# A decoder layer on one core: projections in two halves of the tokens, with the gated recurrence woven into them

## The reference

```python
h = rmsnorm(x, norm_gain) * (1 + scale[:, None]) + shift[:, None]
qa, ka, va, za, qb, fb, ib, zb, ga, gb = jnp.split(h @ w_in, cuts, axis=-1)
# branch A: dilated window attention, three groups (dilation 1, 4, 16), with RMS-normed q and k
branch_a = (o_a * jax.nn.silu(za)) @ w_ba
# branch B: gated recurrence, 4 heads, forget dim 128, value dim 128
f = lbh + (1.0 - lbh) * jax.nn.sigmoid(fb)
o_b, s_new = hgrn2_recurrence(jax.nn.silu(qb), 1.0 - f, ib, jnp.log(f), hgrn_state)
branch_b = (rmsnorm(o_b, o_gain) * jax.nn.silu(zb)) @ w_bb
merged = jax.nn.sigmoid(ga) * branch_a + jax.nn.sigmoid(gb) * branch_b
y = x + gate[:, None] * (merged @ w_o)
```

## Time and profile before

| | us |
|---|---|
| median of 3 runs | 3477.08 |
| profiled execution | 3473.88 |
| its span | 3472.1 |
| PE busy / DVE / ACT / POOL | 3033.0 / 1518.9 / 840.6 / 679.0 |
| mean granted clock of PE | 0.925 |

### The profile page before, as it was taken

One profiled execution on the slowest core, in us unless ns is written; L12 is line 12 of the kernel. 1 busy time (PEld: TensorE's weight loads), 2 busy tenths in 40 slices (PEclk: granted clock), 3 DMA queues, 4 the chain that ended last, 5 costly groups with the idle time before them and its releaser, 6 DMA issues. The chain is left out here.

```text
span 3472.1 us, 45359 instructions
## 1 busy us (share of the span) xinstructions
PE 3033.0 (87%) x17964; PEld 2737.5 (79%) x17964; DVE 1518.9 (44%) x2895; ACT 840.6 (24%) x1646; POOL 679.0 (20%) x662
## 2 busy tenths in 40 slices
PE   7499999999999999999999689898555566569999
PEld 7499999999999999999998456666344545459999
DVE  2687111111111114876666334343466766644343
ACT  1311000013333332111111345344222222222010
POOL 0311111024454543111110002112022222222000
PEclk9999999999999999999999799897777767779999
DMA  5212223221212212221221868767322020035333
GB/s 178 91 59 75 75 57 76 64 69 63 78 66 78 83 55 90 75 75 59 75 72 51 304 222 263 259 210 255 112 88 76 1 76 26 1 124 166 111 120 97
DMA packets 246786, 362.19 MB, mean 104 GB/s; under 512 B 22704, under 2 KB 183728, under 8 KB 230192
## 3 DMA queue, kind: packets, MB, share of 16 engines
q1 hardware_dynamic: 239664, 350.64, 31.4%
q10 hardware_dynamic: 6912, 8.65, 0.7%
HBM read 237.45 MB, written 121.79 MB: 103 GB/s over the span
## 5 line engine op out<-in xcount | busy, mean ns | idle before, releaser
L495 PE MATMUL project_bank<-h_high,project_w_high 128*128 128x448 f32 (+1 forms) x2240 | 795.0, 355 | 28.3 <-POOL project_w_low L585 28.3
L496 PE MATMUL project_bank<-h_low,project_w_high 128*128 128x448 f32 (+1 forms) x2240 | 794.8, 355 | 0.0
L497 PE MATMUL project_bank<-h_high,project_w_low 128*128 128x448 f32 (+1 forms) x2240 | 794.7, 355 | 0.0
L495 PEld LDWEIGHTS project_bank<-h_high,project_w_high 128*128 128x128 f32 x2240 | 421.3, 188 | 53.7 <-issue 28.4
L496 PEld LDWEIGHTS project_bank<-h_low,project_w_high 128*128 128x128 f32 x2240 | 421.1, 188 | 25.5
L497 PEld LDWEIGHTS project_bank<-h_high,project_w_low 128*128 128x128 f32 x2240 | 421.1, 188 | 24.9
L585 POOL TENSOR_TENSOR project_w_low<-project_w_raw,project_w_high 128x512 fp32r<-128x512 f32 x144 | 185.0, 1290 | 771.6 <-ACT project_w_high L539 771.6
L509 PE MATMUL project_bank<-project_w_high,h_low 128*128 128x256 f32 x1088 | 307.9, 283 | 0.0
L508 PE MATMUL project_bank<-project_w_low,h_high 128*128 128x256 f32 x1088 | 307.9, 283 | 0.0
L507 PE MATMUL project_bank<-project_w_high,h_high 128*128 128x256 f32 x1088 | 307.9, 283 | 0.0
L642 DVE SCALAR_TENSOR_TENSOR project_out<-project_bank,project_gains,project_rstd 128x448 f32<-128x448 f32 (+2 forms) x120 | 89.0, 742 | 404.0 <-ACT project_rstd L556 404.0
(11 more groups left out here) (188 smaller groups left out, 4642.7 us busy)
## 6 DMA issues: line engine op xcount, KB each, us to landing
mix_kv<-in_kT_c SPq DMA_DIRECT2D x24, 1024.0 KB, 7.5
mix_kv<-in_v_c SPq DMA_DIRECT2D x24, 1024.0 KB, 7.1
project_w_raw<-in_w_qkv SPq DMA_DIRECT2D x72, 256.0 KB, 4.9
scratch_gates<-project_out SPq DMA_DIRECT2D x16, 1056.0 KB, 4.5
tail_gates<-scratch_gates SPq DMA_DIRECT2D x48, 352.0 KB, 3.2
scratch_sums<-mix_o_out SPq DMA_DIRECT2D x48, 264.0 KB, 6.0
mix_rows<-scratch_sums SPq DMA_DIRECT2D x24, 528.0 KB, 7.0
scratch_v_rows<-project_out SPq DMA_DIRECT2D x24, 520.0 KB, 6.8
```

Source lines behind the costliest of these rows:

```text
L495: pe.matmul(dst, w_high[:, s, k, :], h_high[:, k, tok], start=(k == 0), stop=False)
L496: pe.matmul(dst, w_high[:, s, k, :], h_low[:, k, tok], start=False, stop=False)
L497: mm = pe.matmul(dst, w_low[:, s, k, :], h_high[:, k, tok], start=False, stop=(k == KD - 1))
```

## The change

The features of half of the tokens are in SBUF at a time (`h_high` and `h_low` have 1088 columns in the place of 2112). phase_input makes the second half first and stores it to DRAM (`store_h`, two DMAs for each of three chunks, six in all, 8.9 MB), then the first half over it; ACT, DVE and POOL wait for the stores whose columns they write over.

`phase_weave` takes the place of phase_project and of phase_hgrn, which is gone. It runs the list of jobs twice, once for each half of the tokens, in chunks of 512 or of 384, 352 and 352 columns, two jobs of a weight pair taking turns; the weights are loaded and split in each half. Between the halves SP loads the stored features (`load_features`). The first 14 jobs of a half are those that feed the recurrence. From then on each unit has a slot number, and at each slot every engine does, after its part of the unit, what `recurrence(s, k)` has for it: a step s of the recurrence begins every 13 slots (9 after a sample step) and is spread over slots -5 to 17 counted from its start. All operations of the recurrence and their shapes stay; its inputs go through DRAM as before. Its PSUM needs four banks; the banks of the projections are 3 in the place of 5, those of the head sums 1 in the place of 2. POOL's cast of the squares goes to DVE (`high_squares`), DVE's reciprocal to ACT: the curve is now exp(-log(1 + exp(-u))), with DVE's clamp and maximum around it. q and k of the dilations 4 and 16 are stored by SP in pieces of 256 or 64 elements (`by_group`), since each half has only a part of each residue's row.

```diff
+    CHUNK = ((1024, 384), (1408, 352), (1760, 352), (0, 352), (352, 336), (688, 336))
...
+                def store_h(c):
+                    sp.wait_ge(low_a_done, c + 1)
+                    sp.wait_ge(low_b_done, c + 1)
+                    sp.dma_start(dr["h_half"][0, :, :, cols(c)], h_high[:, :, cols(c)].bitcast(F32)).then_inc(h_stored[c], 16)
+                    sp.dma_start(dr["h_half"][1, :, :, cols(c)], h_low[:, :, cols(c)].bitcast(F32)).then_inc(h_stored[c], 16)
...
                     load_x(c)
+                    store_h(c - XBUF)
...
+def phase_weave(nc, t, dr):
...
+    HALF = SEQ // 2
+    CHUNKS_OF = (((0, 512), (512, 512)), ((1024, 384), (1408, 352), (1760, 352)))
+    ORDER = ([("query", 0, 0), ("forget", 0, 0), ("query", 1, 0), ("forget", 1, 0), ("input", 0, 0), ("z", 4, 0), ("z", 5, 0),
+              ("query", 2, 0), ("forget", 2, 0), ("query", 3, 0), ("forget", 3, 0), ("input", 1, 0), ("z", 6, 0), ("z", 7, 0)]
+             + [("value", g, m) for m in range(2) for g in range(G)]
+             + [(kind, g, jp) for jp in range(PAIRS) for g in range(G) for kind in ("q", "k")]
+             + [("z", n, 0) for n in range(4)] + [("gate", b, m) for m in range(8) for b in range(2)])
+    FIRST_JOBS = 14
+    JOBS = [(half, *job) for half in range(2) for job in ORDER]
     ROWS, NORMED, CURVED = ("value", "input"), ("q", "k"), ("query", "forget", "z", "gate")
-    RAW, RING, BANKS = 3, 3, 5
+    RAW, RING, BANKS = 3, 5, 3
...
+    HSTEPS = [(h, j) for h in range(BH) for j in (0, 1)] + [(h, j) for h in range(BH) for j in (2, 3, 4)]
+    LEVELS = [7 if j < 4 else 3 for h, j in HSTEPS]
...
+        T0 = []
+        for s, (h, j) in enumerate(HSTEPS):
+            if s in (0, 2 * BH):
+                T0.append(5 if s == 0 else HALF_SLOTS + 5)
+            else:
+                T0.append(T0[-1] + (13 if big(s - 1) else 9))
+        END = T0[-1] + 14
...
+            return [(s, T - T0[s]) for s in range(len(HSTEPS)) if -5 <= T - T0[s] <= 17]
...
+            return [4 * (pair + 1) + i for i in ((0, 1), (2,), (3,))[pos]] if pos < 3 and pair + 1 < NPAIR else []
 
...
+                def load_features(c):
+                    lo, w = CHUNKS_OF[1][c][0] - HALF, CHUNKS_OF[1][c][1]
+                    last = pair_first[NPAIR // 2] - (2 if c == 0 else 0)
+                    sp.wait_ge(unit_done, last)
+                    sp.dma_start(h_high[:, :, lo:lo + w].bitcast(F32), dr["h_half"][0, :, :, lo:lo + w]).then_inc(h_in[c], 16)
+                    sp.dma_start(h_low[:, :, lo:lo + w].bitcast(F32), dr["h_half"][1, :, :, lo:lo + w]).then_inc(h_in[c], 16)
...
+                    by_group = lambda dst: dst.rearrange("p (r x) -> p r x", r=DIL[x])[:, :, lo // DIL[x]:(lo + HALF) // DIL[x]]
+                    rows = lambda src: src[:, 0:HALF].rearrange("p (r x) -> p r x", r=DIL[x])
...
-                        sp.dma_start(dr["qT_s"][y, x], a[:, SEQ:NT]).then_inc(done, 16)
+                        sp.dma_start(by_group(dr["qT"][x, y]), rows(a)).then_inc(done, 16)
...
+                    for p in pieces_at(U):
+                        if p + 3 < 2 * len(WEIGHTS):
+                            load(p + 3)
+                    if U == pair_first[NPAIR // 2] - 2:
+                        load_features(0)
+                    if U == pair_first[NPAIR // 2] - 1:
+                        load_features(1)
+                        load_features(2)
+                    if U in slot_of:
+                        for s, k in active(slot_of[U]):
+                            recurrence(s, k)
...
-                for U, (j, u) in enumerate(STEPS):
-                    if u == 0:
-                        pe.wait_ge(w_low_done, 2 * (TILE[j] + (2 if JOBS[j][0] in ROWS else 1)))
+                pe.wait_ge(const_in, 112)
+                for U, (j, c) in enumerate(STEPS):
+                    half, kind = JOBS[j][:2]
+                    if U == pair_first[pair_of(U)]:
+                        pe.wait_ge(w_low_done, 4 * (pair_of(U) + 1))
+                    if U - pair_first[NPAIR // 2] in (0, 2, 4):
+                        pe.wait_ge(h_in[(U - pair_first[NPAIR // 2]) // 2], 32)
                     if U >= BANKS:
                         pe.wait_ge(evac_done, U - BANKS + 1)
-                    if JOBS[j][0] in ROWS:
+                    if kind in ROWS:
...
+                    if U and is_a("normed", U - 1):
                         head_sums(U - 1)
+                    if U in slot_of:
+                        for s, k in active(slot_of[U]):
+                            recurrence(s, k)
...
+                def logarithm(U):
+                    n, e = NTH["curved", U], curve_part(U)
+                    act.wait_ge(clamp_done, n + 1)
+                    act.activation(e, e, ACT.Exp, scale=-1.0).then_inc(eu_done, 1)
+                    act.wait_ge(eu_done, n + 1)
+                    act.activation(e, e, ACT.Ln, bias=1.0).then_inc(log1_done, 1)
+                def sigmoid(U):
+                    n, e = NTH["curved", U], curve_part(U)
+                    act.wait_ge(larger_done, n + 1)
+                    act.activation(e, e, ACT.Exp, scale=-1.0).then_inc(sig_done, 1)
...
+                for U in range(len(STEPS)):
+                    if is_a("normed", U):
                         square(U)
-                    elif JOBS[j][0] in CURVED:
-                        exponential(U)
-                    if U and normed(U - 1):
+                    if is_a("curved", U):
+                        logarithm(U)
+                    if U and is_a("normed", U - 1):
                         root(U - 1)
+                    for p in pieces_at(U):
+                        split_high(p)
+                    if U in slot_of:
+                        for s, k in active(slot_of[U]):
...
+                for U, (j, c) in enumerate(STEPS):
+                    if is_a("ones", U):
+                        ones_column(j, c // 2)
+                    if is_a("normed", U):
+                        low_squares(U)
+                    for p in pieces_at(U):
+                        split_low(p)
+                    if U in slot_of:
+                        for s, k in active(slot_of[U]):
+                            recurrence(s, k)
...
+                def high_squares(U):
+                    n, w = NTH["normed", U], width(*STEPS[U])
...
+                def clamp(U):
+                    j, c = STEPS[U]
...
+                    dve.tensor_scalar(e, u, -40.0, None, ALU.max).then_inc(clamp_done, 1)
+                def larger(U):
+                    e, u = curve_part(U)
+                    dve.wait_ge(log1_done, NTH["curved", U] + 1)
+                    dve.scalar_tensor_tensor(out=e, in0=u, scalar=-1.0, in1=e, op0=ALU.mult, op1=ALU.max).then_inc(larger_done, 1)
...
+                for U in range(len(STEPS) + 1):
+                    if U and is_a("curved", U - 1):
+                        leave_curve(U - 1)
+                    if is_a("curved", U):
+                        clamp(U)
+                    if is_a("normed", U):
+                        high_squares(U)
+                    if U in slot_of:
+                        for s, k in active(slot_of[U]):
+                            recurrence(s, k)
+                    if U and is_a("normed", U - 1):
+                        norm(U - 1)
+                    if is_a("curved", U):
+                        larger(U)
+                    if U < len(STEPS) and JOBS[STEPS[U][0]][1] in ROWS:
                         copy_rows(U)
...
-def phase_hgrn(nc, t, dr):
...
+    dr["h_half"] = nc.dram_tensor("scratch_h_half", (2, P, KD, SEQ // 2 + NS), F32).ap()
...
-            keep(ctx, "h_high", [P, KD, NT], F32R)
-            keep(ctx, "h_low", [P, KD, NT], F32R)
+            keep(ctx, "h_high", [P, KD, SEQ // 2 + NS], F32R)
+            keep(ctx, "h_low", [P, KD, SEQ // 2 + NS], F32R)
             phase_input(nc, t, dr)
-            phase_project(nc, t, dr)
+            phase_weave(nc, t, dr)
         phase_mix(nc, t, dr)
-        phase_hgrn(nc, t, dr)
```

More of the change, by code:

```diff
@@ L123, in _ @@
                 sp.wait_ge(ident_in, 16)
+                for c in range(3):
+                    sp.wait_ge(h_stored[c], 32)
             @block.tensor
@@ L377, in phase_project @@
[L377 to L385 removed]
+                return (2, 2, 2)[:2 + half]
+            if kind == "k" and x == 0:
+                return (3,) if half else (1,)
+            if natural(half, kind, x):
+                return (1 + half, 1)
@@ new lines, in stores_of @@
+            return (1 + half,) if kind == "q" else (1,)
+        TILE, WEIGHTS, SLOT, FREE, AFTER = [], [], [], [], []
+        totals, slot = [0] * RING, 0
+        for job in JOBS:
+            TILE.append(len(WEIGHTS))
+            WEIGHTS += [weight(*job, i) for i in range(2 if job[1] in ROWS else 1)]
+            SLOT.append([]), FREE.append([]), AFTER.append([])
+            for n in stores_of(*job):
+                SLOT[-1].append(slot % RING)
+                FREE[-1].append(totals[slot % RING])
```

(37 more changed lines are left out.)

1119 lines of the change are left out of this document (560 added, 559 removed).

## The result

The changed kernel takes 3145.19 us (median of 4 runs, 3143.97 to 3148.44) against 3477.12 for the kernel before: a ratio of 0.904, with a 95% interval of 0.902 to 0.906.

What follows compares the result with a forecast made beforehand. PE's matmul columns bound the projections, a chain of short hand-overs the recurrence. 3472.1 - 568.7 + 211 + 42 + 14 + 6 + 8 = 3184 us, with 1.8 and 3.2 us added 3189; range 3122 to 3300.

Steps and rivals of the forecast that it cites:

- The phase that goes: Recurrence phase between projections and mix: its 568.7 us leave the span.
- PE's work in the recurrence: Recurrence matmuls, all added on PE behind the projections' units: 211 us, bounds 205 and 235.
- The projections' own matmuls: Projection matmuls on PE, same columns in other pieces: no change, at most 1% (17 us) more.
- Slots and SP queue: Woven stage: late scaled keys at weight pairs' first slots, 22 us; weight pieces held behind 256 B stores on SP, 20.
- Input: Input phase: feature stores on SP delay the last w_ada pieces and x loads, 14 us, bounds 5 and 36.
- Start: Woven stage's start: PE waits for four split pieces, four more constants ahead of the weights: 6 us, bounds 4 and 9.
- Middle: Between the halves: PE stalls while 8.9 MB of features are loaded back, 8 us, bounds 0 and 17.
- Rival (a): Woven stage: PE still waits 1.03 us for each of 224 recurrence groups, 231 us, kernel 3378 us; chance 0.17.
- (b): SP queue: the small stores hold the weights in full, 186 us instead of 20, kernel 3355 us; chance 0.08.
- (c): Woven stage: waits in each slot lower PE's clock, at 0.71 kernel 3986 us, slower than before; chance 0.05.
- (d): End of the woven stage: the recurrence is not covered and its slots trail behind the last unit; chance 0.02.

Runs made afterwards that it cites:

- e4: Changed kernel with all the recurrence's slots moved behind the last unit of the projections, same order inside, none under a unit: 3391.8 us.
- e5: Changed kernel with three more unused 128x512 operations on DVE ahead of the recurrence's part in each slot: 3289.4 us.
- e1: Changed kernel without the recurrence's arithmetic on PE, DVE, ACT and POOL and its loads of forget gates, queries and values: 2908.6 us.
- x_pool: Changed kernel with the recurrence's part of a slot ahead of the next weights' splits on POOL and ACT, not behind them: 3134.3 us.
- e3: Changed kernel with q and k stored as one 4 KB stretch a partition per half instead of pieces of 64 or 256 elements: 3146.6 us.
- e2: Changed kernel with PE taking each of 124 level products one slot earlier, no projection unit between maker and reader of its operands: 3696.1 us.

## Why the prediction was right, step by step

The mechanism was the forecast one: the phase went, its matmuls came to PE, and the hand-overs stayed behind. The sum was 44 us too high, from sizes that partly cancel; the largest part is the 42 us for slots and the SP queue, of which 15.3 came.

- **The phase that goes**, 568.7: right, but the prediction took it as one cost. Run e4 shows that 95 us of it were waits between steps, which the new order removes even without the weave. The prediction's chain of short hand-overs (84.8 us) was not the phase's largest wait: that was the 104.2 us at the starts of steps. And DVE was not nearly idle in the projections (698 of 1753 us), but what it had left sufficed (e5).
- **PE's work in the recurrence**: 211 forecast, 198.5 measured, with the 18.0 us that are counted at the units behind it (e1); below the lower bound of 205. The price of a product was right (0.2225 forecast, 0.223 between starts inside a group). Two terms of a step were mis-sized. The four transposes are single matmuls of 0.11 us, and the sum has each at the 0.2225 of a pair. And the sums over 512 columns were taken from a row's duration, 1.13 us; they delay the unit behind them by 0.87 (558.74 to 559.84 is 1.10, less the usual 0.227 of a unit's matmul). A step thus takes 11.1 us, not 11.8. The sample steps (22) were right at 21.

```profile
558.74 1.02 PE L771 MATMUL weave_kd<-weave_hsq,weave_ones_i 128*128 128x512 f32 x2
559.20 0.80 PE L680 MATMUL weave_bank<-h_high,weave_w_high 128*128 128x512 f32 x1
559.84 0.39 PE L681 MATMUL weave_bank<-h_low,weave_w_high 128*128 128x512 f32 x1
```

- **The projections' own matmuls**: 0 forecast, minus 3.7 measured (plus 14.3 start to start, less the 18.0 that belong to the recurrence). That it came out near nothing is luck: minus 25.4 in the new pieces and plus 21.7 beside the recurrence (lower clock 9, seams 4.9, the rest ahead of the groups and spread out). Neither was in the sum.
- **Slots and SP queue**: 22 and 20 forecast, 15.3 and nothing measured. The place in the slots was right (POOL's splits, run x_pool), and the lower clock behind two of the waits adds some 5 us, which stand among the projections above. The queue's term took a load of 512 B rows, landed after 11.6 us, as the price of the small stores; they landed after 4.0 to 4.5 and hold nothing up (e3). ACT's late pieces of weights (34.4 us, 11 times) reached no wait of PE.
- **Input**: 14 forecast, 10.2 measured. Of the other profiles with the same input, e3 has 165.0 us too, and six have 166.8 to 168.7, which is 11.9 to 13.8 more than before, so the forecast was nearer than this one profile says. PE stood as foreseen at the w_ada piece behind the stores:

```profile
133.36 3.58 PE L160 MATMUL input_gate_ps<-input_c_act,input_w_ada 128*128 128x9 f32 x16 [22.55 <-DMA input_w_ada<-in_w_ada]
```

- **Start**: 6 forecast, 6.4 measured (first load to first unit 14.2 us, 7.8 before).
- **Middle**: 8 forecast, 12.4 measured, and 2 more at the lower clock behind it. The prediction named the queue behind the features' loads, but not the one ahead: on SP two weight pieces were held first, so that the first features left at 1090.60, when PE had all but run out (the last matmul of the first half starts at 1091.3).

```profile
1084.86 5.69 SPq L524 DMA_DIRECT2D weave_w_raw<-in_w_b  x2
1090.60 0.57 SPq L531 DMA_DIRECT2D h_high<-scratch_h_half  x1
```

- The rest: the stage's end is 1.8 us shorter, mix and tail 3.5 longer, and median and span lie 0.9 us apart, not 5.
- **Rival (a)** did not come, and e2 shows its condition and its price: without the unit of lead 551 us, more than the 231 that I gave it, as a wait is 4 us there and not 1.03, and the clock falls too. **(b)** fell with e3, **(c)** with the clock of 0.99; e2 at 0.91 is the nearest to it. **(d)** did not occur.

## What to carry to other kernels

When a chain of short hand-overs is put under an engine that is full, count the work it adds there start to start inside a group, at the clock it will have, and give every operand one whole unit of that engine's time between maker and reader: here the lead was worth 551 us, more than the weave. Where one kind of work gives way to another, add both intervals before calling one of them dear: here 18.0 of 22.9 us at the seams belonged to the other side. Look afterwards at the load that is queued behind held ones and at the order of duties inside a slot: they were worth 6 and 14 us of PE's waits. Test the weave against the same order without it, since part of the gain (here 85 of 332 us) may come from the order and the halves alone.

## What the runs showed of the hardware

- A projection matmul behind a group of the recurrence took 0.112 us longer to the next start (204 places, no wait in the trace), and the last product of 128 columns ahead of it had only 0.03 us to its start, where inside a group it had 0.11. Over all places the two leave 4.9 us.
- In after the clock fell inside a full stage too: behind each of the four sample steps, whose outputs are 16 matmuls of 8 columns, the 352-column matmuls behind the first one went from 0.16 to 0.29 us between starts, though PE had not stood idle. Each stretch cost about 1.6 us. In x_pool it came behind three of the four. It did so behind the 12.4 us idle at the middle as well (0.32 at 384 columns, 2.3 us), and behind two of the waits for POOL, of 2.51 and 1.78 us. Behind two others of 1.78 and 1.84 us the granted clock stayed at 1.00.

```profile
1516.32 1.95 PE L763 MATMUL weave_o<-weave_q_in,weave_s 128*128 128x8 f32 x16
...
1518.37 0.32 PE L681 MATMUL weave_bank<-h_low,weave_w_high 128*128 128x352 f32 x1
1518.53 0.45 PE L682 MATMUL weave_bank<-h_high,weave_w_low 128*128 128x352 f32 x1
1518.78 0.50 PE L680 MATMUL weave_bank<-h_high,weave_w_high 128*128 128x352 f32 x1
```

```profile
1907.95 1.11 PE L729 MATMUL weave_kd<-ident,weave_k_out 128*128 128x128 f32 x4 [2.51 <-POOL weave_k_out L951]
...
1909.74 0.50 PE L680 MATMUL weave_bank<-h_high,weave_w_high 128*128 128x352 f32 x1
1910.03 0.49 PE L681 MATMUL weave_bank<-h_low,weave_w_high 128*128 128x352 f32 x1
```

- Stores of 512 KB in 2048 pieces of 256 B landed after 4.0 to 4.5 us, in pieces of 1 KB after 3.2, in pieces of 4 KB after 2.6; the stage took 1982.3 us with the small pieces and 1982.6 without.
